# The first two weight chunks worked through together, piece by piece, and x loaded from a second queue

## The chip, the core and the metric

The kernel runs on one core of one Trainium2 chip. The metric is device time in microseconds (us) of one execution. The kernel before took 962.37 us (median of three runs, 961.73 to 966.79).

## What is computed

One layer of a streaming encoder on x, 512 tokens by 1024 channels, in float32. Cut to its shape:

```
proj = x @ w_in                       # 1024 columns in; queries, keys, values of four mixers, four gates out
o_a = top-k gathered softmax attention, chosen by an indexer (aiq, aik, aiw)
o_b = chunked attention with clipped relative bias
o_c = sliding window attention with sinks
o_d = stick-breaking attention
y   = sum over the four of sigmoid(gate_i) * (o_i @ w_branch_i)
x   = layer_norm(ALPHA * x + y @ w_out)
x   = layer_norm(ALPHA * x + (silu(hg) * hu) @ w_ffn_out)      # hg, hu = x @ w_ffn_in
```

## The kernel before

**Weights as a stream.** All weights come as 71 chunks of 1 MB, `stream[c]`, each 128 partitions by 2048 floats. A chunk of the input projection holds 256 output columns for all eight 128-row tiles of the contraction (`KT` = 8), 256 floats (`CW`) for each. Chunk 0 (`iq`) and chunk 1 (`ikck`) make indexer queries and keys, chunk 2 (`cvw`) values, chunk 3 `aq`, 4 `ak`, 5 `av`, 6 `dq`, and so on. Slot t is the work on chunk t.

**Three products for one.** For accuracy each float32 operand is split in two. ScalarE copies a chunk to `w_hi`, rounded (`high`, line 467); VectorE subtracts to get `w_lo` (`low`, line 701); TensorE multiplies hi by hi, hi by lo and lo by hi (`PARTS`). A chunk of the input projection is 48 matmuls: 2 output tiles, 8 contraction tiles, 3 parts. x itself is split once in the same way, into `x_hi` (line 597) and `x_lo` (line 856).

**Two buffers.** `raw`, `w_hi` and `w_lo` have two halves, chunk c in half c % 2. This makes a ring of waits:

- SyncE issues the load of chunk c into `raw` (line 353) once `low(c-2)` has read the half;
- ScalarE starts `high(c)` once the load has landed (`raw_loaded`) and once TensorE is done with chunk c-2 (`wait_used`, which waits for the last output tile of that chunk in `tile_done`);
- VectorE starts `low(c)` after `high(c)`, TensorE its slot c after `low(c)`.

On ScalarE each slot t does `high(t + 1)` ahead of emptying the output banks of chunk t (`empty_tile`, line 498 and others).

**The start.** Chunk 0 and x are cut in five `PIECES` along the contraction: tiles 0, 1, then 2-3, 4-5, 6-7. SyncE issues a piece of chunk 0 (line 342) and the same piece of x (line 343) in turn, ten DMAs, then chunk 1 whole (line 344). ScalarE and VectorE split piece by piece (lines 595, 597, 854, 856). TensorE first runs 11 matmuls on zeros (`WARM_UP`), and then chunk 0 tile by tile of the contraction (`first_chunk`, line 1051). Chunk 1 comes after it as an ordinary slot (`slot_half`, line 1027). The load of chunk 2 waits for the last `w_lo` piece of chunk 0, that of chunk 3 for `low(1)`.

**Beside it.** GpSimd computes small bias vectors and writes them to DRAM, every row repeated 128 times: `vec_t5` from 8 partitions (line 406, 2560 KB) and `vec_rel` from 4 partitions (line 407, 1280 KB). When both have landed it reads them back as bias tiles (line 411). These stores share the DMA engines with the weight stream.

The waits that order the loads in SyncE's loop:

```python
if j:
    sp.wait_ge(lo_ready, c - 1)
else:
    sp.wait_ge(first_lo_ready, len(PIECES))
    sp.wait_ge(lo_ready, c - 2)
```

The functions that the change touches:

Of the kernel before, what the change touches and what calls it, by code (L numbers as in the profile page):

```python
# [20 lines left out]
P = 128  # L21
# [14 lines left out]
KT = D_MODEL // P  # L36
TOK = SEQ // P
CHUNK_COLS = 2048
CW = CHUNK_COLS // KT
# [18 lines left out]
N_SLOTS = len(SLOTS)  # L58

PIECES = [(0, 1), (1, 2)] + [(k, k + 2) for k in range(2, KT, 2)]  # L60
OUT0 = N_SLOTS
FIN0 = OUT0 + 4
# [96 lines left out]
def layer_program(nc, stream, xT, x, t5T, relR, sinks, g1c, b1c, g1, b1, g2, b2, out):  # L159
# [96 lines left out]
    with ctx:  # L256
# [3 lines left out]
        def sem(name):  # L260
            return ctx.enter_context(nc.semaphore(name))

        raw_loaded = [sem("raw_loaded_even"), sem("raw_loaded_odd")]
        first_loaded = [sem(f"first_loaded{i}") for i in range(len(PIECES))]
        first_hi_ready, first_lo_ready = sem("first_hi_ready"), sem("first_lo_ready")
        x_loaded = [sem(f"x_loaded{i}") for i in range(len(PIECES))]
        sink_loaded, resid_loaded = sem("sink_loaded"), sem("resid_loaded")
        ln1_loaded, ln2_loaded, cols_loaded = sem("ln1_loaded"), sem("ln2_loaded"), sem("cols_loaded")
# [70 lines left out]
        @block.sync  # L339
        def _(sp):  # L340
            for i, (k, end) in enumerate(PIECES):
                sp.dma_start(raw[:, 0, CW * k:CW * end], stream[0, :, CW * k:CW * end]).then_inc(first_loaded[i], 16)
                sp.dma_start(xraw[:, k:end, :], xT[:, k:end, :]).then_inc(x_loaded[i], 16)
            sp.dma_start(raw[:, 1, :], stream[1]).then_inc(raw_loaded[1], 16)
            with sp.Fori(2, N_CHUNKS - 1, 2) as c:
                for j in range(2):

# [5 lines that stand above are left out]
                    sp.dma_start(raw[:, j, :], stream[bass.ds(c + j, 1)].rearrange("a p n -> p (a n)")).then_inc(raw_loaded[j], 16)  # L353
            for tok in range(TOK - 1):
                sp.wait_ge(out_ready, tok + 1)
                sp.dma_start(out[tok * P:(tok + 1) * P, :], result[:, tok, :]).then_inc(stored, 16)
            sp.wait_ge(out_ready, TOK)
            sp.dma_start(out[P * (TOK - 1):, 0:512], result[:, TOK - 1, 0:512]).then_inc(stored, 16)
            sp.wait_ge(stored, 16 * (TOK + 1))
# [90 lines left out]
        def _(act):  # L450
# [10 lines left out]
            def high(c):  # L461

                s = c % 2
                act.wait_ge(raw_loaded[s], 16 * ((c + 1) // 2))
                if c >= 2:
                    wait_used(act, c - 2)
                act.activation(w_hi[:, s, :], raw[:, s, :], ACT.Copy).then_inc(hi_ready, 1)  # L467
# [105 lines left out]
            def stack_high(n):  # L573
# [14 lines left out]
                act.activation(k_stack[rows, :], k[rows, :], ACT.Copy)  # L588
                act.activation(k_stack[others, :], k[rows, :], ACT.Copy).then_inc(stack_hi_ready, 1)

            act.preload_act_table_set("natural_log_exp_and_others")
            for i, (k, end) in enumerate(PIECES):
                s = slice(CW * k, CW * end)
                act.wait_ge(first_loaded[i], 16)
                act.activation(w_hi[:, 0, s], raw[:, 0, s], ACT.Copy).then_inc(first_hi_ready, 1)
                act.wait_ge(x_loaded[i], 16)
                act.activation(x_hi[:, k:end, :], xraw[:, k:end, :], ACT.Copy).then_inc(x_hi_ready, 1)
            for t in range(N_SLOTS):
                before, now = UNIT_AT.get(t - 1), UNIT_AT.get(t)
                if now is not None and UNITS[now][:2] == ("D", 0):  # L600
                    act.wait_ge(consts_ready, 1)
                    for rounded, mask in ((neg_tri_r, neg_tri), (neg_all_r, neg_all)):
                        act.activation(rounded[:], mask[:], ACT.Copy)
                if before is not None and UNITS[before][0] != "I":
                    unit_stage2(before)
                high(t + 1)
                if t == N_SLOTS - 1:
                    for k in range(EARLY):
                        y_high(k)
                stack_high(UNIT_AT.get(t + 1))  # L610
                if now is not None:
                    unit_stage1(now, before)
                else:
                    unit_out(before)
                if SLOTS[t][0] != "W":
                    empty_tile(t, 0)
                if SLOTS[t] == ("W", BRANCH_ORDER[-1]):
                    for j in range(EARLY, 8):
                        empty_tile(t, j)
                elif SLOTS[t][0] != "W" and t < N_SLOTS - 1:  # L620
                    empty_tile(t, 1)
# [33 lines left out]
            def high_of(c, s, loads, used, count):  # L655

                act.wait_ge(raw_loaded[s], loads * 16)
                act.wait_ge(used, count)
                act.activation(w_hi[:, s, :], raw[:, s, :], ACT.Copy).then_inc(hi_ready, 1)  # L659

            def ffn_pair(p, parity, first=False, early=False):
                if first:
                    high(FIN0 + 1)
                else:
                    high_of(FIN0 + 1 + 2 * p, (FIN0 + 1) % 2, p + (FIN0 + 2) // 2, up_done, 2 * p)
                for j in range(2):
                    act.wait_ge(gate_done, 2 * p + (j + 1))
                    if not first:
                        act.wait_ge(h_lo_ready, 2 * p + (j - 1))
                    act.activation(swi[:, j, :], banks[4 * parity + j][:], ACT.Tanh, scale=0.5).then_inc(tanh_ready, 1)  # L670
                high_of(FIN0 + 2 + 2 * p, FIN0 % 2, p + (FIN0 + 3) // 2, gate_done, 2 * p + 2)
                for j in range(2):
                    act.wait_ge(hidden_ready, 2 * p + (j + 1))
                    act.activation(h_hi[:, bass.ds(2 * p + j, 1), :], swi[:, j:j + 1, :], ACT.Copy).then_inc(h_hi_ready, 1)  # L674
# [11 lines left out]
        def _(dve):  # L686
# [164 lines left out]
            for i, (k, end) in enumerate(PIECES):  # L851
                s = slice(CW * k, CW * end)
                dve.wait_ge(first_hi_ready, i + 1)
                dve.tensor_tensor(w_lo[:, 0, s], raw[:, 0, s], w_hi[:, 0, s].bitcast(f32), ALU.subtract).then_inc(first_lo_ready, 1)
                dve.wait_ge(x_hi_ready, i + 1)
                dve.tensor_tensor(x_lo[:, k:end, :], xraw[:, k:end, :], x_hi[:, k:end, :].bitcast(f32),
                                  ALU.subtract).then_inc(x_lo_ready, 1)
            for t in range(N_SLOTS):
                before, now = UNIT_AT.get(t - 1), UNIT_AT.get(t)
                if now is not None and UNITS[now][0] == "A":  # L860
                    mask_unit(now)
                branch = BRANCH_ORDER.index(SLOTS[t][1]) if SLOTS[t][0] == "W" else None
                if branch is None:
                    low(t + 1)
                last_branch = branch == len(BRANCH_ORDER) - 1
                if branch is not None:
# [148 lines left out]
        def _(pe):  # L1015
# [23 lines left out]
                    e = EMPTIED_BY[g - 4]  # L1039
                    pe.wait_ge(act_emptied if e == "act" else dve_emptied, emptied_before(e, g - 4) + 1)  # L1040

            def first_chunk():

                for k in range(KT):
                    piece = next(i for i, (_, end) in enumerate(PIECES) if k < end)
                    pe.wait_ge(first_lo_ready, piece + 1)
                    pe.wait_ge(x_lo_ready, piece + 1)
                    for j in range(2):
                        w = columns(0, P * j, P, CW)
                        for n, (a, b) in enumerate(PARTS):  # L1050
                            ins = pe.matmul(prod[j][:], w[a](k), x_all[b](k), start=k == 0 and n == 0,  # L1051
                                            stop=k == KT - 1 and n == len(PARTS) - 1)
                        if k == KT - 1:
                            ins.then_inc(tile_done, 1)

            def slot_half(t, half, between=None):
                kind, what = SLOTS[t]
# [100 lines left out]
            pe.wait_ge(warm_ready, 1)  # L1158
            for _ in range(WARM_UP):
                pe.matmul(obank[:], warm[:, 0:P], warm[:], start=True, stop=True)  # L1160
            first_chunk()
            for t in range(1, N_SLOTS):
                before, now = UNIT_AT.get(t - 1), UNIT_AT.get(t)
                if before is not None and UNITS[before][0] != "I":
                    unit_stage2(before)
                pe.wait_ge(lo_ready, t)

                def units():
                    if now is not None:
                        unit_scores(now)  # L1170
                    if before is not None and UNITS[before][0] != "I":
                        unit_values(before)

                slot_half(t, 0, units)
                slot_half(t, 1)
# [146 lines left out]
```

## Time and profile before

| | |
|---|---|
| median of three runs | 962.37 us |
| span of the profiled execution, first to last instruction | 957.6 us |
| TensorE (PE) busy | 900.7 us, 94% |
| VectorE (DVE) busy | 466.3 us, 49% |
| ScalarE (ACT) busy | 339.7 us, 35% |
| GpSimd (POOL) busy | 56.0 us, 6% |
| mean granted TensorE clock | 0.967 |
| chain that ended last, by engine | PE 82%, DMA 9%, DVE 6%, ACT 1%, issue 1% |

The profiled execution is known by its span; 4.8 us lie between it and the median of the timed runs. In the rows below, times are us from the span's start, L is a line of the kernel, PEld is the weight load of TensorE, and SPq is SyncE's queue. "[2.50 <-DVE x_lo L856]" means that the engine stood idle for 2.50 us and that this instruction of DVE ended the wait. "DMA to landing" is the time from issue until the last byte has landed. q1 is the hardware queue that SyncE issues to, q0 the queue of GpSimd.

### The profile page before, as it was taken

What the parts mean: (1) busy time and instruction counts of PE and PEld (TensorE: products, weight loads), DVE (VectorE), ACT (ScalarE), POOL (GpSimd) and SP (SyncE); (2) the same over time, 40 slices, a digit from 0 to 9 for tenths busy, and PEclk for the clock granted to TensorE, in tenths of its full rate; (3) what the DMA queues carried; (4) which work ended last, traced back from release to release, by engine and by line L of the source; (5) the groups of instructions that cost most, each with busy time, mean ns of one, the idle gap of its engine ahead of it and who ended that gap; (6) DMA issues with size and microseconds to landing.
All of it is one profiled execution on the core that took longest, in us unless ns stands there. A gap on an engine that the chain in (4) does not pass through costs nothing.

```text
span 957.6 us, 10388 instructions
## 1 busy us (share of the span) xinstructions
PE 900.7 (94%) x4079; PEld 718.4 (75%) x4079; DVE 466.3 (49%) x742; ACT 339.7 (35%) x503; POOL 56.0 (6%) x92
## 2 busy tenths in 40 slices
PE   7949499999999999999999986999999999999996
PEld 5836478787777777777788864888888888888885
DVE  4204159878554753963628259334333444312217
ACT  4203236666453544453234152232222322212112
POOL 8000010000000000000000028000000000000001
PEclk9977799999999999999999997999999999999998
DMA  7876472112111311221222611322232222322212
GB/s 230 116 92 93 61 255 88 44 45 85 48 44 48 105 68 45 88 88 44 88 89 95 229 73 39 137 88 89 94 124 89 88 88 89 117 102 88 88 45 88
DMA packets 16168, 88.93 MB, mean 93 GB/s; under 512 B 2940, under 2 KB 3200, under 8 KB 7296
## 3 DMA queue, kind: packets, MB, share of 16 engines
q1 hardware_dynamic: 11952, 77.34, 22.5%
q0 software_dynamic: 4032, 10.78, 7.8%
q8 instruction: 28, 0.46, 0.2%
q10 hardware_dynamic: 144, 0.26, 0.1%
q14 instruction: 12, 0.10, 0.0%
HBM read 82.33 MB, written 6.03 MB: 92 GB/s over the span
## 4 chain that ended last, share of the span: by engine, by line
PE 82%; DMA 9%; DVE 6%; ACT 1%; issue 1%; POOL 0%; SPq 0%; DVEq 0%; POOLq 0%
PE bank L1027 54%; PE bank L1182 16%; DMA raw<-in_stream 9%; PE bank L1153 4%; PE bank L1111 2%; DVE x_lo L959 2%; PE bank L1110 2%; PE bank L1140 1%; DVE w_lo L701 1%; PE bank L1127 1%; PE bank L1051 1%; DMA xraw<-in_xT 1%; DVE x1t L955 1%; ACT w_hi L467 1%; PE bank L1099 1%; PE bank L1244 1%
## 5 line engine op out<-in xcount | busy, mean ns | idle before, releaser
L701 DVE TENSOR_TENSOR w_lo<-raw,w_hi 128x2048 fp32r<-128x2048 f32 x69 | 158.1, 2291 | 268.9 <-ACT w_hi L467 246.3
L1027 PE MATMUL bank<-x_hi,w_hi 128*128 128x512 f32 x720 | 188.2, 400 | 29.7 <-DVE w_lo L701 28.7
L1027 PEld LDWEIGHTS bank<-x_hi,w_hi 128*128 128x128 f32 x720 | 134.7, 191 | 60.2 <-DVE w_lo L701 29.3
L1027 PE MATMUL bank<-x_lo,w_hi 128*128 128x512 f32 x720 | 179.8, 392 | 0.0
L1027 PE MATMUL bank<-x_hi,w_lo 128*128 128x512 f32 x720 | 178.3, 390 | 0.0
L1027 PEld LDWEIGHTS bank<-x_lo,w_hi 128*128 128x128 f32 x720 | 136.3, 189 | 29.1
L1027 PEld LDWEIGHTS bank<-x_hi,w_lo 128*128 128x128 f32 x720 | 135.6, 188 | 28.3
L467 ACT ACTIVATE w_hi<-raw 128x2048 fp32r<-128x2048 f32 x48 | 92.0, 1917 | 181.5 <-PE bank L1182 94.9
L1182 PE MATMUL bank<-w_lo,h_hi 128*128 128x512 f32 x176 | 56.8, 389 | 0.0
L1182 PE MATMUL bank<-w_hi,h_lo 128*128 128x512 f32 x176 | 56.8, 389 | 0.0
L1182 PE MATMUL bank<-w_hi,h_hi 128*128 128x512 f32 x176 | 56.7, 389 | 0.0
L486 ACT ACTIVATE gates<-bank 128x512 f32<-128x512 f32 x30 | 17.9, 598 | 90.7 <-PE bank L1027 84.1
L674 ACT ACTIVATE h_hi<-swi 128x512 f32 (+1 forms) x22 | 13.9, 632 | 95.5 <-DVE swi L971 95.5
L670 ACT ACTIVATE swi<-bank 128x512 f32<-128x512 f32 x22 | 13.2, 599 | 89.4 <-PE bank L1027 70.5
L971 DVE SCALAR_TENSOR_TENSOR swi<-swi,bank 128x512 f32<-128x512 f32 x22 | 15.1, 687 | 60.6 <-PE bank L1027 60.6
L965 DVE SCALAR_TENSOR_TENSOR swi<-swi,bank 128x512 f32<-128x512 f32 x22 | 15.1, 687 | 54.8 <-ACT swi L670 54.8
L659 ACT ACTIVATE w_hi<-raw 128x2048 fp32r<-128x2048 f32 x21 | 40.0, 1905 | 0.0
L1182 PEld LDWEIGHTS bank<-w_hi,h_lo 128*128 128x128 f32 x176 | 33.0, 188 | 6.9
L1182 PEld LDWEIGHTS bank<-w_lo,h_hi 128*128 128x128 f32 x176 | 33.0, 188 | 6.8
L1182 PEld LDWEIGHTS bank<-w_hi,h_hi 128*128 128x128 f32 x176 | 33.0, 188 | 6.8
L706 DVE SCALAR_TENSOR_TENSOR gates<-gates,bank 128x512 f32<-128x512 f32 x22 | 14.6, 684 | 31.4 <-PE bank L1027 31.2
L543 ACT ACTIVATE probs<-probs,neg_max 128x256 f32<-128x256 f32 (+3 forms) x48 | 25.1, 525 | 10.5 <-DVE neg_max L814 10.2
(213 smaller groups left out, 1083.6 us busy)
## 6 DMA issues: line engine op xcount, KB each, us to landing
raw<-in_stream SPq DMA_DIRECT2D x69, 1024.0 KB, 4.8
bias_vectors<-vec_t POOLq DMA_DIRECT2D x1, 2560.0 KB, 55.1
resid<-in_x POOLq DMA_DIRECT2D x1, 2048.0 KB, 8.2
xraw<-in_xT SPq DMA_DIRECT2D x3, 512.0 KB, 7.6
out<-result SPq DMA_DIRECT2D x3, 512.0 KB, 3.1
bias_vectors<-vec_rel POOLq DMA_DIRECT2D x1, 1280.0 KB, 102.6
bias_b<-bias_vectors POOLq DMA_DIRECT2D x1, 1024.0 KB, 6.0
bias_a<-bias_vectors POOLq DMA_DIRECT2D x1, 1024.0 KB, 12.0
```

The source lines that it names most:

```text
L467: act.activation(w_hi[:, s, :], raw[:, s, :], ACT.Copy).then_inc(hi_ready, 1)
L486: ins = act.activation(gates[:, 2 * quarter + j, :], src[:], ACT.Tanh, scale=0.5)
L543: last = act.activation(probs[:, s], probs[:, s], ACT.Exp, bias=neg_max[:, r:r + 1], accum_out=row_sum[:, r:r + 1])
L659: act.activation(w_hi[:, s, :], raw[:, s, :], ACT.Copy).then_inc(hi_ready, 1)
L701: dve.tensor_tensor(w_lo[:, s, :], raw[:, s, :], w_hi[:, s, :].bitcast(f32), ALU.subtract).then_inc(lo_ready, 1)
L959: dve.tensor_tensor(x_lo[:, k, :], x1t[:, k, :], x_hi[:, k, :].bitcast(f32), ALU.subtract).then_inc(x1_lo_ready, 1)
L965: dve.scalar_tensor_tensor(swi[:, j, :], swi[:, j, :], 1.0, banks[4 * parity + j][:], ALU.add, ALU.mult).then_inc(gated, 1)
L1027: ins = pe.matmul(dst, lhs[a](k), rhs[b](k), start=n == 0, stop=n == n_all - 1)
L1110: pe.matmul(dst, q_stack[:, queries], k_stack[:, k0:k0 + width], start=True, stop=False)
L1111: ins = pe.matmul(dst, q_stack[rows, queries], k_low[rows, k0:k0 + width], start=False, stop=True)
L1153: ins = pe.matmul(obank[rows, q0:q0 + width], value_head(kind, h, kb), probsT[:, b * 512 + col:b * 512 + col + width], start=kb == 0, stop ...
L1182: return pe.matmul(banks[2 * tok + half][:], left[a][:, k, P * tok:P * (tok + 1)], (w_hi, w_lo)[b][:, (c0 + j) % 2, first:first + 512], st ...
```

## The change

Chunks 0 and 1 are both cut in `PIECES`. SyncE issues the ten pieces in turn, chunk 0 then chunk 1 of each; the five pieces of x are issued by ScalarE ahead of its table load. ScalarE and VectorE split, for each piece, chunk 0, x and chunk 1. TensorE goes along the contraction once and does both chunks at each tile of it. `high(1)`, `low(1)` and slot 1 fall away from the loops; the last piece of chunk 1 counts as `hi_ready` and `lo_ready` 1. Since chunk 1 no longer counts in `raw_loaded[1]`, the waits for odd chunks count one load less.

```diff
         @block.sync
             for i, (k, end) in enumerate(PIECES):
-                sp.dma_start(raw[:, 0, CW * k:CW * end], stream[0, :, CW * k:CW * end]).then_inc(first_loaded[i], 16)
-                sp.dma_start(xraw[:, k:end, :], xT[:, k:end, :]).then_inc(x_loaded[i], 16)
-            sp.dma_start(raw[:, 1, :], stream[1]).then_inc(raw_loaded[1], 16)
+                for c in range(2):
+                    sp.dma_start(raw[:, c, CW * k:CW * end], stream[c, :, CW * k:CW * end]).then_inc(first_loaded[c][i], 16)
...
         @block.scalar
+            for i, (k, end) in enumerate(PIECES):
+                act.dma_start(xraw[:, k:end, :], xT[:, k:end, :]).then_inc(x_loaded[i], 16)
             act.preload_act_table_set("natural_log_exp_and_others")
             for i, (k, end) in enumerate(PIECES):
                 s = slice(CW * k, CW * end)
-                act.wait_ge(first_loaded[i], 16)
+                act.wait_ge(first_loaded[0][i], 16)
                 act.activation(w_hi[:, 0, s], raw[:, 0, s], ACT.Copy).then_inc(first_hi_ready, 1)
                 act.wait_ge(x_loaded[i], 16)
                 act.activation(x_hi[:, k:end, :], xraw[:, k:end, :], ACT.Copy).then_inc(x_hi_ready, 1)
+                act.wait_ge(first_loaded[1][i], 16)
+                act.activation(w_hi[:, 1, s], raw[:, 1, s], ACT.Copy).then_inc(
+                    hi_ready if end == KT else second_hi_ready, 1)
...
-                high(t + 1)
+                if t:
+                    high(t + 1)
...
         @block.vector
                                   ALU.subtract).then_inc(x_lo_ready, 1)
+                if end == KT:
+                    dve.wait_ge(hi_ready, 1)
+                else:
+                    dve.wait_ge(second_hi_ready, i + 1)
+                dve.tensor_tensor(w_lo[:, 1, s], raw[:, 1, s], w_hi[:, 1, s].bitcast(f32), ALU.subtract).then_inc(
+                    lo_ready if end == KT else second_lo_ready, 1)
...
-                if branch is None:
+                if branch is None and t:
                     low(t + 1)
...
         @block.tensor
-            def first_chunk():
+            def first_chunks():
                 for k in range(KT):
                     piece = next(i for i, (_, end) in enumerate(PIECES) if k < end)
+                    for c in range(2):
+                        if c == 0:
+                            pe.wait_ge(first_lo_ready, piece + 1)
+                            pe.wait_ge(x_lo_ready, piece + 1)
+                        elif piece == len(PIECES) - 1:
+                            pe.wait_ge(lo_ready, 1)
+                        else:
+                            pe.wait_ge(second_lo_ready, piece + 1)
+                        for j in range(2):
+                            w = columns(c, P * j, P, CW)
+                            for n, (a, b) in enumerate(PARTS):
+                                ins = pe.matmul(prod[2 * c + j][:], w[a](k), x_all[b](k), start=k == 0 and n == 0,
+                                                stop=k == KT - 1 and n == len(PARTS) - 1)
+                            if k == KT - 1:
+                                ins.then_inc(tile_done, 1)
...
-            first_chunk()
-            for t in range(1, N_SLOTS):
+            first_chunks()
+            for t in range(2, N_SLOTS):
```

## Rows read from the trace of the kernel before

**Rows 1.** The page's busy times of the engines.
```profile
PE 900.7 (94%) x4079; PEld 718.4 (75%) x4079; DVE 466.3 (49%) x742; ACT 339.7 (35%) x503; POOL 56.0 (6%) x92
```

**Rows 2.** The page's chain that ended last, by line, and one of its DMA issues.
```profile
PE bank L1027 54%; PE bank L1182 16%; DMA raw<-in_stream 9%; PE bank L1153 4%; PE bank L1111 2%; DVE x_lo L959 2%; PE bank L1110 2%; PE bank L1140 1%; DVE w_lo L701 1%; PE bank L1127 1%; PE bank L1051 1%; DMA xraw<-in_xT 1%; DVE x1t L955 1%; ACT w_hi L467 1%; PE bank L1099 1%; PE bank L1244 1%
...
bias_vectors<-vec_rel POOLq DMA_DIRECT2D x1, 1280.0 KB, 102.6
```

**Rows 3.** That chain in order of time, 0 to 180: start, length, what.
```profile
23.74 1.92 ACT w_hi L467
25.68 2.30 DVE w_lo L701
...
28.14 41.44 DMA raw<-in_stream
...
74.01 40.68 DMA raw<-in_stream
```

**Rows 4.** Timeline, 36 to 160: TensorE's two restarts. Start, length, engine, line.
```profile
73.90 2.92 PE L1027 MATMUL bank<-x_hi,w_hi 128*128 128x512 f32 x6 [15.90 <-DVE w_lo L701]
...
119.00 2.93 PE L1027 MATMUL bank<-x_hi,w_hi 128*128 128x512 f32 x6 [12.81 <-DVE w_lo L701]
```

**Rows 5.** Instructions of the tile xraw (ns min/median/max, starts), then timeline, 0 to 60.
```profile
L343 SPq DMA_DIRECT2D xraw<-in_xT x5: 425/432/2365, 1.3 to 7.1; - x5
...
9.41 0.63 ACT L595 ACTIVATE w_hi<-raw 128x512 fp32r<-128x512 f32 x1 [1.22 <-DMA raw<-in_stream]
...
13.19 0.47 PE L1051 MATMUL bank<-x_hi,w_hi 128*128 128x512 f32 x1 [2.50 <-DVE x_lo L856]
...
14.73 1.06 ACT L597 ACTIVATE x_hi<-xraw 128x1024 fp32r<-128x1024 f32 x1 [0.44 <-DMA xraw<-in_xT]
...
17.24 1.92 ACT L467 ACTIVATE w_hi<-raw 128x2048 fp32r<-128x2048 f32 x1 [1.46 <-DMA raw<-in_stream]
...
22.82 0.39 PE L1051 MATMUL bank<-x_hi,w_lo 128*128 128x512 f32 x1
...
23.20 1.16 POOL L406 DMA_DIRECT2D bias_vectors<-vec_t  x1 [0.30 <-POOL vec_rel L402]
...
33.71 1.08 PEld L1027 LDWEIGHTS bank<-w_hi,x_hi 128*128 128x128 f32 x8
```

**Rows 6.** Groups by line and shape, 0 to 17: the splits of 512 and 1024 columns.
```profile
L856 DVE TENSOR_TENSOR x_lo<-xraw,x_hi 128x1024 fp32r<-128x1024 f32 x3 | 3.7, 1226 | 1.4 <-ACT x_hi L597 1.4
L597 ACT ACTIVATE x_hi<-xraw 128x1024 fp32r<-128x1024 f32 x3 | 3.2, 1058 | 1.5 <-DMA xraw<-in_xT 1.5
L854 DVE TENSOR_TENSOR w_lo<-raw,w_hi 128x512 fp32r<-128x512 f32 x3 | 2.1, 684 | 1.2 <-ACT w_hi L595 1.2
L595 ACT ACTIVATE w_hi<-raw 128x512 fp32r<-128x512 f32 x3 | 1.9, 619 | 1.2 <-DMA raw<-in_stream 1.2
```

**Rows 7.** Line 353 by stretches: the loads of chunk 3 and of chunk 5.
```profile
L353 SPq DMA_DIRECT2D raw<-in_stream x1: 342/342/342, 21.7 to 21.7; - x1
DMA to landing us min/median/max: 4.9/4.9/4.9
...
L353 SPq DMA_DIRECT2D raw<-in_stream x1: 332/332/332, 39.0 to 39.0; - x1
DMA to landing us min/median/max: 44.8/44.8/44.8
```

**Rows 8.** DMA queues: 34 to 40 (first), 60 to 66 (two), 84 to 88 (last).
```profile
q0 software_dynamic: 60, 0.31, 69.6%
...
q0 software_dynamic: 62, 0.32, 65.4%
q1 hardware_dynamic: 32, 0.26, 10.3%
...
q0 software_dynamic: 21, 0.11, 47.8%
```

**Rows 9.** Windows: busy time by engine, granted clock, DMA share, GB/s of one stretch.
```profile
13.80:17.20 3.40, 3.40 (x10) 2.62 (x9) 3.05 (x3) 1.54 (x2) 3.00 (x6) 0.50 0.69 216
```

More of the change, by code:

```diff
@@ L263, in layer_program @@
         raw_loaded = [sem("raw_loaded_even"), sem("raw_loaded_odd")]
-        first_loaded = [sem(f"first_loaded{i}") for i in range(len(PIECES))]
+        first_loaded = [[sem(f"first_loaded{c}_{i}") for i in range(len(PIECES))] for c in range(2)]
         first_hi_ready, first_lo_ready = sem("first_hi_ready"), sem("first_lo_ready")
+        second_hi_ready, second_lo_ready = sem("second_hi_ready"), sem("second_lo_ready")
         x_loaded = [sem(f"x_loaded{i}") for i in range(len(PIECES))]
@@ L463, in high @@
                 s = c % 2
-                act.wait_ge(raw_loaded[s], 16 * ((c + 1) // 2))
+                act.wait_ge(raw_loaded[s], 16 * (c // 2))
                 if c >= 2:
@@ L670, in ffn_pair @@
                     act.activation(swi[:, j, :], banks[4 * parity + j][:], ACT.Tanh, scale=0.5).then_inc(tanh_ready, 1)
-                high_of(FIN0 + 2 + 2 * p, FIN0 % 2, p + (FIN0 + 3) // 2, gate_done, 2 * p + 2)
+                high_of(FIN0 + 2 + 2 * p, FIN0 % 2, p + (FIN0 + 2) // 2, gate_done, 2 * p + 2)
                 for j in range(2):
@@ L1040, in bank_free @@
                     pe.wait_ge(act_emptied if e == "act" else dve_emptied, emptied_before(e, g - 4) + 1)
-            def first_chunk():
+            def first_chunks():
                 for k in range(KT):
                     piece = next(i for i, (_, end) in enumerate(PIECES) if k < end)
[L1046 to L1054, printed above, removed]
+                    for c in range(2):
[13 more added lines that the diff above has]
+                                ins.then_inc(tile_done, 1)
             def slot_half(t, half, between=None):
```

## The prediction

> **What bounds the kernel now.** I read the busy times first: TensorE is busy for 900.7 of 957.6 us [rows 1]. So a start that feeds it sooner ought to pay, if nothing between start and end can swallow what it gains. The chain of waits by line says that something can: 9% of the span hangs on weight loads [rows 2]. In order of time these are two loads only. Chunk 4 is issued at 28.14 and takes 41.44 us; chunk 6 is issued at 74.01 and takes 40.68 us [rows 3]. TensorE stands idle for 15.90 us before it restarts on chunk 4 at 73.90, and for 12.81 us before chunk 6 at 119.00 [rows 4]. After that no load stands in the chain, so whatever moves the restart at 119.00 moves the end by as much.
>
> Why do they take 41 us when chunk 3, issued at 21.7, took 4.9 [rows 7]? GpSimd issues its bias vector stores from 23.20 on [rows 5]. From 34 to 40, with chunk 4's load outstanding, q0 holds 70% of the DMA time and q1 moves nothing; from 60 to 66 q0 moves 62 packets and q1 32 [rows 8]. A load issued into these stores waits long and then gets its packets between theirs. So what matters is when chunk 4 is issued. That is the end of a ring: TensorE ends chunk 0 (its last matmul starts at 22.82 [rows 5]), `high(2)` may overwrite its half of `w_hi` from 23.74, `low(2)` runs from 25.68, and then SyncE may issue chunk 4 [rows 3].
>
> By the trace q0's share is 65 to 70% until 66 and 48% at 84 to 88 [rows 8], as if the store from 8 partitions and the one from 4 held engines of their own, 12 of 16 and later 8. The Trainium skill's "DMA: Bandwidth & Descriptors", "Why a DMA increments its semaphore by 16 and not by 1", states this: a DMA uses the largest number of engines up to 16 that divides its slowest dimension. The trace agrees. It enters no term below.
>
> **The change, part by part.**
>
> *Matmuls.* None is added. Chunks 0 and 1 are 96 matmuls in both orders. From 22.82 to 33.71 TensorE does one last matmul of chunk 0 and the 48 of chunk 1 [rows 5], less one step: 0.227 us each.
>
> *When the pieces are ready.* TensorE restarts at 13.19 on the third piece (tiles 2-3) [rows 5]. I take it that the third piece decides again: behind it lie six tiles, 72 matmuls, 16.3 us, and pieces four and five are ready in time (ScalarE needs 0.62 + 1.06 + 0.62 us for each and VectorE 0.68 + 1.23 + 0.68 [rows 6], 2.6 us against 5.4 us of matmuls). The third piece is ready when its chunk 0 part and its x have landed and been split: landing L plus 0.62 + 1.06 + 1.23 [rows 6], 2.95 us with the hops.
>
> *L.* The bytes are the same, 4 MB. By the rows 1024 KB had landed at 9.41 (third piece of chunk 0), 3072 KB at 14.73 (last of x), all 4096 KB at 17.24 [rows 5], so 385 KB per us between the first two. Ahead of the third piece now lie chunk 1's first two pieces, and x runs beside the weights on a second queue. If both queues move bytes alike, 768 KB of each: 1536 KB, L = 10.7. If they take turns packet by packet, x, whose rows are twice as long or more, gets ahead: all of x (2048 KB) and 768 KB of weights, 2816 KB, L = 14.1. While the bias stores run, q1 and q0 do seem to take turns by packet [rows 8], which speaks for the later end. Against it I set up to a microsecond for the 2.37 us that one of SyncE's ten issues took, where the others took 0.43 [rows 5]; with five of them on ScalarE's queue this should shorten. I take L = 13.0. ScalarE loses about 2.2 us for its own five issues (0.43 us each) before the table load; its first activation is late by 1 us or so, which the wait for the third piece hides.
>
> The Trainium skill, in the same page under "Queues, rings and completion order", says that an engine round-robins between the queues with work at packet granularity; by it alone L is 14.1 and the sum 1.1 us larger. Under "Issuing engines are not separate DMA queues" it says that issuing from two engines saves only issue time, no bandwidth; this speaks against the change.
>
> *TensorE through both chunks.* The third piece is ready at 13.0 + 2.95 = 15.95. Then 16.3 us of matmuls, and the clock: after its 2.50 us of idling TensorE ran from 13.80 to 17.20 at a granted clock of 0.50, 1.2 GHz [rows 9]; 36 matmuls took 9.86 us from 13.19, 1.7 more than 36 x 0.227. I charge the same 1.7 once. Bounds: nothing, if the doubled work on pieces one and two fills the gap, or twice that, as it now has a longer gap. Both chunks end at 15.95 + 16.3 + 1.7 = 34.0. Before, chunk 1 ended at 33.71 [rows 5]. The gain of interleaving (12 matmuls, 2.7 us, move into idle time ahead of the third piece) is spent on the later piece.
>
> *What is worse.* Chunk 0 is no longer done 48 matmuls before chunk 1, but 6. Its last matmul starts 7 steps before 34.0, at 32.4, not at 22.82. Everything on the ring goes with it by 9.6 us: `high(2)` at 33.3, `low(2)` from 35.3 to 37.6, chunk 4's load at 37.7. TensorE, done at 34.0, waits 3.6 us for `low(2)`, a wait that did not exist before. Behind `high(2)` on ScalarE are queued the emptying of chunk 1's banks and `high(3)`; slots 2 and 3 lasted from 33.71 to 58.0, where the idling before 73.90 began [rows 4, 5], and these 24.3 us hide both.
>
> *Chunks 2 and 3.* Chunk 2 is issued after chunk 0's last `w_lo` piece, chunk 3 after chunk 1's. The splits after L = 13.0 take 7 us on ScalarE plus VectorE's tail, so chunk 3 goes out at 21.5 to 23, as now at 21.7; it still lands ahead of the stores. Cost nothing; if it does not, see the third rival.
>
> *Chunk 4 to chunk 6.* The wait in the stores is what the rows price: 41.44 and 40.68 us, for issues at different phases, 28 and 74. So chunk 4 lands at 79.2, TensorE restarts at 83.5, and chunk 6 is issued at 83.6 and lands at 124.3. Chunk 5, issued after `low(3)` about 41, lands 14.2 us after chunk 4 as before (39.0 + 44.8 against 69.6 [rows 3, 7]) and is in time. TensorE restarts on chunk 6 at 128.6, not 119.0. GpSimd's bias tiles are not read before slot 10, so they give nothing back, and nothing after is late next: the rest is TensorE's.
>
> *Sum.* 957.6 + 9.6 = 967.2 us of span; with the 4.8 us that lie between span and median of the runs, 972.0.
>
> Bounds of the shift. Below: TensorE fed without a gap from about 6.5 us (my estimate, from ScalarE's later first activation) needs 96 x 0.227 = 21.8, an end at 28.3 and a shift of 4; with L = 10.7 and no clock loss it is 5.5. Above: L = 14.1, a second stretch at half clock (1.7), 0.5 for a late ScalarE: 12.9. The later store lands 102.6 us after its issue behind 23.20 [rows 2, 5], at 127, after which a load no longer waits, so it can hardly grow much beyond.
>
> **The rivals.**
>
> 1. *A load issued later waits less* (faster). Perhaps 41 us is the price of a load that meets the stores' beginning, and one issued at 37.7, in their steady state, gets its turn at once, like chunk 5, which needed 14.2 us behind chunk 4. Then chunk 4 lands at about 55, TensorE goes through slots 2 and 3 until 62 and on without waiting, 12 us earlier than 73.90; if chunk 6 still takes 40.7 us from its issue at 62, TensorE restarts at 107: 12 us faster, 950. It decides in this direction once chunk 4 waits under 32 us. Against it: chunk 6, issued in the steady state, took 40.68.
> 2. *The landing is fixed by the stores, not by the issue* (no change). Chunk 4 then lands near 69.6 wherever it is issued before 45, and TensorE restarts at 73.90 and 119.00: 962. For it: no packet of q1 from 34 to 40. Against: the two waits are alike to 0.8 us though their ends lie 45 us apart.
> 3. *Chunk 3 meets the stores.* Issued after 24 it would land at 65; slot 3 ends at 83, chunk 6 is issued about 84 and lands at 125: 10 to 13 us slower, 974.
> 4. *Even pieces* (L near 10.7, clock kept): the mechanism of the forecast with a shift of 4 to 6, 967.
> 5. *The change does not do what it says*: the fine interleaving is in the program order of TensorE, so only the early landing can fail; that is inside the bounds of L.
>
> **How the numbers follow.** Forecast 0.58 (shift 6 to 13), rival 4 0.16, rival 3 0.06, rival 2 0.10, rival 1 0.07, others 0.03. Half a per cent, 4.8 us, is about what a measurement can tell from no change. Faster by more than that: rival 1, 0.08. Within it: rival 2 and the lowest tenth of rival 4 with others, 0.14. Slower: 0.78. The range reaches from just above rival 2, 963, to 977, the upper bound 975.3 with the spread of the runs; outside are rival 1, most of rival 2 and a few per cent above.
>
> **What would show it.** In the changed profile: TensorE's last matmul of the first two chunks near 34 and chunk 0's `tile_done` just before; an idle time of 3 to 4 us of TensorE ahead of slot 2; chunk 4 issued near 37.7 with 41 us to landing; restarts near 83.5 and 128.6; the rest of the trace equal to before but shifted. A landing of chunk 4 in under 32 us, or near 69.6, would make the prediction wrong at the fourth step; an end of the first chunks before 30 would make its size wrong.

## The result

The changed kernel takes 970.0 us (median of 20 runs, 966.66 to 978.33), the kernel before 964.61 us (median of 20, 958.68 to 970.85). The ratio is 1.0068, with a 95% interval from 1.0044 to 1.0091: slower by 0.7%, some 6.6 us. The three runs shown ahead of the prediction had a median of 962.37. (One correction to what stands above: the stream has 70 chunks, not 71.)

In the profiled execution the span is 970.1 us, against 957.6. The page of the changed kernel:

```profile
span 970.1 us, 10396 instructions
PE 909.9 (94%) x4079; PEld 727.7 (75%) x4079; DVE 466.8 (48%) x746; ACT 339.7 (35%) x507; POOL 55.9 (6%) x92
...
PE 81%; DMA 10%; DVE 6%; ACT 1%; issue 0%; POOL 0%; SPq 0%; DVEq 0%; POOLq 0%
```

TensorE has the same number of instructions as in [rows 1] but is busy for 9 us more: the same matmuls, slower. The share of loads in the chain rises from 9 to 10%. The chain that ended last, 0 to 200, in order of time (start, length, what), has the pieces of [rows 3] again:

```profile
2.68 10.79 DMA raw<-in_stream
13.50 0.63 ACT w_hi L597
14.13 0.96 ACT x_hi L599
15.11 1.24 DVE x_lo L862
16.48 15.26 PE bank L1069 x66
31.79 0.47 issue
32.27 1.91 ACT w_hi L467
34.20 2.30 DVE w_lo L707
36.66 42.53 DMA raw<-in_stream
79.22 1.92 ACT w_hi L467
81.16 2.30 DVE w_lo L707
83.62 41.04 DMA raw<-in_stream
```

The third piece's weights land at 13.5, its products start at 16.48. 66 matmuls later chunk 0 is complete; ScalarE empties its two banks and then starts `high(2)`. Chunk 4 is issued at 36.66, where [rows 3] has 28.14, and waits 42.53 us. The timeline of TensorE shows three waits for `w_lo`, where [rows 4] has two:

```profile
36.55 1.97 PE L1039 MATMUL bank<-w_hi,x_hi 128*128 128x132 f32 x8 [3.46 <-DVE w_lo L707]
...
128.97 2.93 PE L1039 MATMUL bank<-x_hi,w_hi 128*128 128x512 f32 x6 [14.30 <-DVE w_lo L707]
```

The first is new, ahead of slot 2. The second restart comes 10.0 us later than the 119.00 of [rows 4]. After it something more is lost. The windows (span, busy time by engine with the number of instructions, granted clock, DMA share, GB/s) of the changed kernel after that restart, and below them those of the kernel before:

```profile
129.00:141.30 12.30, 12.07 (x25) 7.82 (x26) 7.34 (x12) 4.88 (x8) 1.54 (x3) 0.51 0.94 352
```

```profile
119.00:123.00 4.00, 3.78 (x8) 2.23 (x8) 3.05 (x5) 1.51 (x4) 0.00 (x0) 0.50 0.85 183
123.00:134.40 11.40, 11.40 (x48) 8.87 (x49) 4.14 (x7) 3.65 (x5) 2.31 (x3) 1.00 0.66 232
```

TensorE had idled in both, and in both it restarted at a granted clock of 0.50, 1.2 GHz. But the kernel before got 2.4 GHz back after 4.0 us, the changed kernel after 12.3. Slot 7 starts at 147.91 instead of 134.36: 13.55 us late, 9.97 of it at the restart and 3.58 at the lower clock. About 1 us comes back by the end. The two spans differ by 12.5 us, the medians of 20 runs by 5.4: part of what this pair of profiles shows belongs to the two executions, and the experiments have to say which part.

### The profile page after: what moved, and what is told of

Same layout as the page of the kernel before. It is cut to its first block, busy times and chain, and to the rows that moved or that the text cites. A ratio compares the mean times of both kernels' runs of the same rounds, so it can differ in the third digit from the quotient of the medians.

```text
span 970.1 us, 10396 instructions
## 1 busy us (share of the span) xinstructions
PE 909.9 (94%) x4079; PEld 727.7 (75%) x4079; DVE 466.8 (48%) x746; ACT 339.7 (35%) x507; POOL 55.9 (6%) x92
## 4 chain that ended last, share of the span: by engine, by line
PE 81%; DMA 10%; DVE 6%; ACT 1%; issue 0%; POOL 0%; SPq 0%; DVEq 0%; POOLq 0%
PE bank L1039 54%; PE bank L1200 15%; DMA raw<-in_stream 10%; PE bank L1171 4%; PE bank L1129 2%; DVE x_lo L971 2%; PE bank L1128 2%; PE bank L1069 2%; PE bank L1158 1%; DVE w_lo L707 1%; PE bank L1145 1%; DVE x1t L967 1%; ACT w_hi L467 1%; PE bank L1117 1%; DVE resid L932 1%; PE bank L1262 0%
## 5 line engine op out<-in xcount | busy, mean ns | idle before, releaser
L707 DVE TENSOR_TENSOR w_lo<-raw,w_hi 128x2048 fp32r<-128x2048 f32 x68 | 155.8, 2292 | 279.7 <-ACT w_hi L467 257.0
L1039 PE MATMUL bank<-x_hi,w_hi 128*128 128x512 f32 x704 | 184.6, 401 | 27.4 <-DVE w_lo L707 26.4
L1039 PE MATMUL bank<-x_lo,w_hi 128*128 128x512 f32 x704 | 175.9, 392 | 0.0
L1039 PEld LDWEIGHTS bank<-x_hi,w_hi 128*128 128x128 f32 x704 | 131.9, 192 | 57.2 <-DVE w_lo L707 27.0
L1039 PE MATMUL bank<-x_hi,w_lo 128*128 128x512 f32 x704 | 174.3, 390 | 0.0
L1039 PEld LDWEIGHTS bank<-x_lo,w_hi 128*128 128x128 f32 x704 | 133.3, 189 | 28.4
L1039 PEld LDWEIGHTS bank<-x_hi,w_lo 128*128 128x128 f32 x704 | 132.6, 188 | 27.7
```

The source lines that it names most:

```text
L707: dve.tensor_tensor(w_lo[:, s, :], raw[:, s, :], w_hi[:, s, :].bitcast(f32), ALU.subtract).then_inc(lo_ready, 1)
L1039: ins = pe.matmul(dst, lhs[a](k), rhs[b](k), start=n == 0, stop=n == n_all - 1)
```

## The experiments

Each kernel is compared with runs of the kernel before on the same chip; ratios are to the kernel before. Where two kernels of different experiments are set side by side below, the kernel before took 964.94, 964.37 and 964.88 us on the three chips used.

**Both kernels once more.** One profile each had been read; how far does a second one differ?

> The kernel before, unchanged, for a second profile of it. Theory A (chunk 4 is issued at a time that the ring of buffers sets, and each load then waits some 41 us in the bias stores): chunk 4 is issued near 28.1, lands after 40 to 43 us, TensorE restarts near 74 and near 119 to 121; the ratio to itself is 1.000. Theory B (what differs from run to run is the clock after the restarts, not the loads): the stretches at a granted clock of 0.5 begin and end at other places than in the first profile, and the span differs from 957.6 by several us though the restarts stand within 2 us of the first profile's.

Measured: 961.84 us against 964.94 of the kernel before, ratio 0.9988 (0.9955 to 1.0021). Its chain, 0 to 180, then TensorE's second restart in the timeline and the window behind it:

```profile
14.83 10.03 PE bank L1051 x36
...
29.79 40.92 DMA raw<-in_stream
...
75.13 40.15 DMA raw<-in_stream
```

```profile
119.59 1.65 PE L1027 MATMUL bank<-x_hi,w_hi 128*128 128x512 f32 x3 [12.28 <-DVE w_lo L701]
```

```profile
119.60:131.00 11.40, 11.17 (x23) 7.12 (x24) 6.35 (x8) 4.56 (x8) 2.32 (x3) 0.50 0.71 200
```

The third piece starts at 14.83, where [rows 5] has 13.19, and chunk 4 goes out at 29.79, not 28.14. The waits of 41 us are the same. The clock stayed at 1.2 GHz for 11.4 us behind the restart, where the first profile had 4.0.

> The changed kernel, unchanged, for a second profile of it. Theory A: chunk 4 is issued at 36 to 38, the restarts come at 83 to 84 and 128 to 130, about 10 us behind the kernel before. If the end moves by much less than 10 us in the timed runs (ratio 1.004 to 1.009), the difference lies after the second restart (clock) or in chunk 6, whose landing the end of the stores near 125 cuts short when the kernel before lands it late. Theory B: the second restart is 10 us late in this profile too and the clock stretches differ from the first profile's by up to 4 us of matmul time.

Measured: 971.35 us, ratio 1.0078 (1.0049 to 1.0107). Its chain:

```profile
36.12 44.85 DMA raw<-in_stream
...
85.39 43.83 DMA raw<-in_stream
```

The issue falls into the expected 36 to 38; the waits are 2 to 3 us longer here and put the second restart at 133.54, later than the expected 128 to 130. It also shows that the end of the stores cuts nothing short. Over two profiles each, chunk 4 is issued at 28.14 and 29.79 before, at 36.66 and 36.12 after: 7.4 us later on the mean, 8.5 in the first pair. As to the clock, three of the four profiles agree and the first one of the kernel before is the exception with its 4.0 us. In after_again the window behind the second restart reads:

```profile
133.50:144.70 11.20, 10.94 (x22) 6.98 (x23) 7.27 (x12) 4.94 (x8) 2.32 (x3) 0.50 0.91 320
```

So the 3.6 us after the restart belong to an execution, not to the kernel. In before_again, though, the restarts do stand within 2 us of the first profile's, as theory B said.

**Without the bias stores.** If the stores are the amplifier, taking them away should leave little of the loss.

```diff
-            pool.dma_start(vec_dram[0:2 * HEADS], vec_t5[:]...).then_inc(vec_stored, 16)
-            pool.dma_start(vec_dram[2 * HEADS:], vec_rel[:]...).then_inc(vec_stored, 16)
-            pool.wait_ge(vec_stored, 32)
...
-                pool.dma_start(tile[:], ...).then_inc(bias_loaded, 16)
-            pool.wait_ge(bias_loaded, 16 * 3)
+            for t in ("B", "C"):
+                pool.memset(bias[t][:], 0.0)
+            step(pool.memset(bias["A"][:], 0.0))
+            step_wait()
```

> The kernel before without the stores of the bias vectors and without reading them back; the bias tiles are filled with zeros, so the outputs are not the reference's. Theory A: no load takes more than 6 us, TensorE does not idle before slots 4 and 6, and 28.7 us of idling and some 10 us at half clock go: 925 to 935 us. Rival (the loads are slow for another reason): under 5 us faster.

Measured: 924.31 us, ratio 0.9588 (0.9555 to 0.9622), just below the expected range. TensorE waits for no `w_lo` of a whole chunk any more, and chunk 4 lands 4.8 us after its issue.

> The same with the changed kernel (no bias stores, zeros in the bias tiles, outputs not the reference's). Theory A: what the change costs without the stores is only the later start of slot 2, near 36 instead of 33.7, since TensorE waits for low(2) for 3.6 us after the first chunks: 1.5 to 3 us slower than the kernel before without stores. Rival (the delay of the ring costs 10 us by itself, stores or not): 8 to 10 us slower than it. Rival that the change was meant for (interleaving gains when loads are fast): 0 to 3 us faster than it.

Measured: 936.51 us. That is 12.2 us slower than before_nostore, and my expectation of 1.5 to 3 was wrong by a factor of four or more. The rival of 8 to 10 us from the ring does not fit either: slot 2 starts at 38.37, 2.5 us behind the 35.88 of before_nostore. The window from there on, in after_nostore, shows the rest:

```profile
38.30:62.10 23.80, 23.73 (x103) 22.63 (x103) 4.40 (x5) 5.44 (x9) 0.00 (x0) 0.50 0.24 89
```

After 3.5 us of waiting TensorE ran at 1.2 GHz for 23.8 us. This I call theory C: the short wait ahead of slot 2 costs more by the clock behind it than by itself. In the changed kernel the same stretch is there; I took it to be hidden, because slots 2 and 3 end before chunk 4 lands in any case (after_fill, below, tests this). The changed kernel's window:

```profile
35.50:59.40 23.90, 22.85 (x102) 22.43 (x103) 4.65 (x4) 3.88 (x6) 0.00 (x0) 0.51 0.81 86
```

**Only the later issue of chunk 4.** The step on which the prediction rests, done alone in the kernel before.

```diff
-            with sp.Fori(2, N_CHUNKS - 1, 2) as c:
+            ...                                    # chunks 2 and 3 as before, written out
+            sp.wait_ge(tile_done, 4)
+            with sp.Fori(4, N_CHUNKS - 1, 2) as c:
```

> The kernel before, with one wait added: SyncE issues chunk 4 only when TensorE has ended chunk 1 (tile_done 4). Nothing else moves. Theory A (the time of chunk 4's issue sets the restarts): chunk 4 is issued at 34 to 36 instead of 28 to 30, lands 41 to 44 us later, both restarts and the end come 5 to 6 us later: ratio 1.005 to 1.006. Rival (landing is fixed by the stores): chunk 4 lands near 70 all the same, ratio 1.000.

Measured: 972.67 us, ratio 1.0071 (1.0035 to 1.0106). Its chain and its second restart:

```profile
35.82 43.20 DMA raw<-in_stream
...
83.45 42.09 DMA raw<-in_stream
```

```profile
129.86 2.93 PE L1032 MATMUL bank<-x_hi,w_hi 128*128 128x512 f32 x6 [14.80 <-DVE w_lo L706]
```

One wait on SyncE, with nothing else changed, costs as much as the whole change: 6.8 us, with an interval from 3.4 to 10.2. The landing moved with the issue, so it is not fixed by the stores. In this profile the second restart is 10 us late and not 5 to 6, because both loads also waited longer, 43.20 and 42.09 us.

**Only TensorE's order undone.**

```diff
-                for k in range(KT):
-                    for c in range(2):
+                for c in range(2):
+                    for k in range(KT):
```

> The changed kernel with one part undone: TensorE does all of chunk 0 and then all of chunk 1; loads, queues and splits stay interleaved. Theory A (the loss comes from chunk 0 ending only 6 matmuls before chunk 1): chunk 0's last matmul starts near 24.5 to 25, high(2) near 25.5, chunk 4 is issued near 30, TensorE does not wait ahead of slot 2, restarts near 76 and 121, time within 2 us of the kernel before: ratio 0.999 to 1.003. Rival (the loads in smaller pieces and the busier ScalarE are what costs): ratio stays at 1.006 or more.

Measured: 965.69 us, ratio 1.0022 (0.9992 to 1.0052), no longer told from the kernel before. Its chain:

```profile
16.59 11.12 PE bank L1069 x36
27.75 0.47 issue
28.22 1.92 ACT w_hi L467
...
32.63 41.18 DMA raw<-in_stream
```

Chunk 4 goes out at 32.63, 2.6 us later than expected: the third piece is ready at 16.59, and its 36 matmuls took 11.12 us instead of 10.0, at half clock for part of it. By the medians the order of the matmuls is the larger part of the loss and the interleaved loads, which make the third piece late, a smaller one; the interval here and that of the change (1.0044 to 1.0091) overlap a little.

Put together, the runs give a series of chunk 4's issue against the ratio:

| kernel | chunk 4 issued | ratio |
|---|---|---|
| before, two profiles | 28.14, 29.79 | 1 (0.9988) |
| after_chunk0_first | 32.63 | 1.0022 |
| before_hold4 | 35.82 | 1.0071 |
| changed, two profiles | 36.66, 36.12 | 1.0068, 1.0078 |
| after_fill (below) | 37.70 | 1.0075 |

From 29 to 36.4 that is 7.4 us of issue for 6.6 to 7.5 us of time. The series is good to some 3 us at each point, not better: every ratio has an interval of about 0.3% to either side, and in the profiles the waits of chunks 4 and 6 in the stores varied between 40.1 and 44.9 us. The longer waits do not go with the later issue: after_fill, with the latest issue of all, has 41.57 and 40.1.

**The stores done otherwise.** If 41 us of waiting come from the way in which the stores go out, in rows of 2.5 KB from 8 and 4 partitions, one wide transfer of the same copies should take it away, with the right outputs.

```diff
-            pool.dma_start(vec_dram[0:2 * HEADS], vec_t5[:].unsqueeze(1).to_broadcast([2 * HEADS, P, VL])).then_inc(vec_stored, 16)
-            pool.dma_start(vec_dram[2 * HEADS:], vec_rel[:].unsqueeze(1).to_broadcast([HEADS, P, VL])).then_inc(vec_stored, 16)
-            pool.wait_ge(vec_stored, 32)
+            pool.dma_start(vec_small[0:2 * HEADS], vec_t5[:]).then_inc(small_stored, 16)
+            pool.dma_start(vec_small[2 * HEADS:], vec_rel[:]).then_inc(small_stored, 16)
+            pool.wait_ge(small_stored, 32)
+            pool.dma_start(vec_dram[:], bass.AP(vec_small.tensor, vec_small.offset, [[0, P], [1, 3 * HEADS * VL]])).then_inc(vec_stored, 16)
+            pool.wait_ge(vec_stored, 16)
```

`vec_dram` is now 128 rows of 12 x 640 floats, and the readback steps by 12 x 640 - 1.

> The kernel before with the bias stores done otherwise: the 12 vectors are stored once (30 KB), and one transfer from DRAM to DRAM, 128 rows of 30 KB, makes the 128 copies, so that no store goes out from 8 or 4 partitions. Same outputs. Theory A: chunk 4 lands in under 20 us, TensorE's idling before slots 4 and 6 goes wholly or nearly, 925 to 940 us. Rival (it is the bytes of the stores, not their few source partitions): the loads stay slow, over 950 us.

Measured: 923.62 us (921.74 to 925.13), ratio 0.9561 (0.9532 to 0.9590). It beats both kernels by over 40 us and is as fast as with no stores at all. Among its DMA issues (what, engine, count, KB, us to landing) is the one that makes the copies:

```profile
bias_vectors<-bias_small POOLq DMA_DIRECT2D x1, 3840.0 KB, 16.3
```

The two stores before needed 102.6 us for the same 3840 KB. [rows 2] puts that time against the 1280 KB alone, but both stores count on one semaphore, so it tells only when the later of them had landed. Chunk 4's load, issued at 29.2 beside the wide transfer, still took 17.0 us instead of 4.8. That costs nothing, because TensorE has slots 2 and 3 to work on meanwhile and the transfer is over soon.

What about the stores was slow? The edit changes three things at once: the engines that the copies are spread over, the bytes in one packet, and the memory that they are read from (DRAM and not SBUF). The queue view separates the first. This is GpSimd's queue from 30 to 36 in before_spread (packets, MB, share of the 16 engines' time):

```profile
q0 software_dynamic: 54, 1.66, 78.3%
```

[rows 8] has 60 packets, 0.31 MB and 69.6% for six microseconds of the old stores. So the queue holds hardly more of the engines' time than before, and its packets take about as long, 1.4 us against 1.1 (share times 16 engines times 6 us, over the packets). But each carries 31 KB and not 5. Even after one of the old stores had landed, when the queue was down to 47.8% [rows 8], the share is a factor of 1.6; the bytes in a packet are a factor of six. The few partitions, and the few engines that go with them, are therefore the smaller part of the slowness. Whether a packet of 5 KB needs 1.1 us for its short rows or for being read from SBUF was not tested.

> The changed kernel with the same other stores. After the runs without stores I expect the changed kernel to be 10 to 13 us slower than before_spread: 2 us of later start of slot 2 and some 10 us of half clock after its 3.5 us wait ahead of slot 2. If the clock stays up, 2 to 3 us slower.

Measured: 938.40 us (935.29 to 939.00), 14.8 us above before_spread, a little more than expected. These two kernels scatter by 4 us, not 12, so the parts can be read. TensorE's timeline at slot 2, first before_spread, then after_spread:

```profile
35.02 1.01 PE L1030 MATMUL bank<-w_hi,x_hi 128*128 128x132 f32 x8
35.86 1.06 PE L1030 MATMUL bank<-w_lo,x_hi 128*128 128x132 f32 x8
```

```profile
39.61 1.83 PE L1042 MATMUL bank<-w_hi,x_hi 128*128 128x132 f32 x8 [3.46 <-DVE w_lo L710]
41.24 1.91 PE L1042 MATMUL bank<-w_lo,x_hi 128*128 128x132 f32 x8
```

Slot 2 starts 4.6 us later, after a wait of 3.46 us, and then eight products take 1.91 us instead of 1.06. The rest, about 10 us, is the stretch that begins there. The window of after_spread:

```profile
39.60:63.50 23.90, 23.89 (x104) 22.75 (x104) 4.69 (x4) 5.66 (x9) 3.90 (x8) 0.50 0.60 222
```

TensorE is busy all the time and has 1.2 GHz.

**The wait filled.** Theory C, tested: TensorE is kept at work through the wait.

```diff
             first_chunks()
+            for _ in range(14):
+                pe.matmul(obank[:], x_hi[:, 0, 0:P], x_hi[:, 0, :], start=True, stop=True)
```

> after_spread with 14 matmuls more, whose result nobody reads, in TensorE's 3.5 us wait ahead of slot 2. They take 14 x 0.227 = 3.2 us, so slot 2 starts as before near 39.6. Theory C (the wait costs 3.5 us itself and 10 to 12 us by the half clock that follows it): the stretch at 0.5 from 39.9 goes, slot 2 takes 10.9 us instead of 20.4, 938.4 falls to 926 to 929 us. Rival (the clock falls for another reason, as slot 2's short matmuls): no change, 938.

Measured: 927.05 us, 11.4 us less than after_spread, by doing more. Its timeline, and the window from 34 on:

```profile
34.64 3.33 PE L1184 MATMUL bank<-x_hi 128*128 128x512 f32 x14
38.26 1.11 PE L1042 MATMUL bank<-w_hi,x_hi 128*128 128x132 f32 x8 [0.29 <-DVE w_lo L710]
39.21 1.06 PE L1042 MATMUL bank<-w_lo,x_hi 128*128 128x132 f32 x8
```

```profile
34.00:60.00 26.00, 25.71 (x159) 21.97 (x158) 10.70 (x10) 12.40 (x18) 3.91 (x8) 1.00 0.92 317
```

The half clock is gone, with the same short matmuls in slot 2, so these did not bring it about. What is left of the change is 3.4 us, and slot 2 starts 3.2 us later than in before_spread.

> The changed kernel, with its bias stores as they are, and the same 14 matmuls more ahead of slot 2. Theory C with theory A: the half clock in slots 2 and 3 goes, but these slots end before chunk 4 lands anyway, so the restarts and the time stay: ratio to the kernel before 1.004 to 1.010. Rival (the half clock is part of the loss that was timed): ratio near 1.000.

Measured: 971.39 us, ratio 1.0075 (1.0047 to 1.0103). Slots 2 and 3 run at full clock (the window), chunk 4 waits 41.57 us as ever (the chain), and TensorE idles for longer instead, 21.84 us ahead of the first restart where the changed kernel has 12.10:

```profile
36.00:60.50 24.50, 24.21 (x152) 20.73 (x151) 5.20 (x4) 4.42 (x7) 0.00 (x0) 1.00 0.80 86
```

```profile
37.70 41.57 DMA raw<-in_stream
```

So in the changed kernel as it stands the half clock at slot 2 costs nothing, and the ring's delay behind the stores is the loss.

**The parts of the change with the wide transfer.**

> after_chunk0_first (loads and splits interleaved, TensorE does chunk 0 first) with the single wide bias transfer. No wait ahead of slot 2, so no half clock after it. Theory C: within 3 us of before_spread's 923.6, on the slow side since the third piece is ready 1 to 2 us later (16.6 against 14.3): 924 to 927. If the interleaved loads themselves cost more, 930 or above.

Measured: 926.07 us (924.99 to 927.54), 2.4 us above before_spread: what the interleaved loads cost when TensorE takes chunk 0 first.

> before_spread with one part of the change alone: x is issued from ScalarE's queue, chunk 1 whole as before. If the queues take turns packet by packet, x gets ahead of chunk 0's pieces, and the third piece (x lands last now, at about 11.9) is ready 1 us earlier to 1 us later: 922.5 to 925. If the second queue brings bandwidth, 921 or below.

Measured: 922.89 us (921.94 to 923.90), 0.7 us below before_spread, within the scatter of both. Its chain has the third piece at work at 12.82, where before_spread has 14.32:

```profile
9.84 0.63 ACT w_hi L599
10.47 0.96 ACT x_hi L601
11.45 1.24 DVE x_lo L860
12.82 10.03 PE bank L1055 x36
```

The second queue for x is thus no part of the loss. That it makes the start earlier is not shown: 1.5 us in one profile, where five profiles with the opening of the kernel before (13.19, 14.83, 14.50, 14.57 and 14.32) differ by 1.6, and 0.7 us in the timed runs.

## Why the prediction was right, point by point

The sign, the mechanism and the range were right. The size was not as right as it looks. The sum was forecast as 972.0 and measured as 970.0, but from another baseline: I forecast a shift of 9.6 us, and the timed runs show 5.4 between the medians and 6.6 by the ratio. The shift was thus 3 to 4 us too large, and the baseline of three runs, 962.37, was 2.2 us below the 964.61 of twenty. That the second error covered half of the first was luck.

- *The ring.* Right. before_hold4 makes a loss of the same size by one wait, and after_chunk0_first undoes most of it by the order of the matmuls alone. Forecast for chunk 4's issue 37.7, measured 36.66 and 36.12.
- *L, and the third piece.* L was taken as 13.0 between 10.7 and 14.1; it was 13.5, and 12.98 in the second profile. By the rule of the Trainium skill's "DMA: Bandwidth & Descriptors", "Queues, rings and completion order" (an engine goes round-robin between its queues, packet by packet) it would have been 14.1; the traces came 0.6 and 1.1 us before that, nearer to it than to 10.7. They also show x ahead, as that end supposes: in the changed kernel ScalarE waits for pieces of the weights only, never for x. My support for it from [rows 8] was misread: 62 packets against 32, and 60 against none, are no turns one for one. The products started at 16.48, not 15.95.
- *The shift of the ring.* This is the term that was mis-sized: 9.6 us forecast, 7.4 measured over two profiles each. At the late end chunk 4's issue came 1.3 us before the 37.7, mostly since the clock's 1.7 us (next point) did not fall due. At the early end I took the third piece's start before as 13.19, from the one profile there was. It is 14.83 in before_again, 14.50 in before_hold4 and 14.32 in before_spread; that first profile caught x early.
- *The clock's 1.7 us.* Charged to the stretch behind the third piece; it did not fall there. The window 11.60 to 15.00 of the changed kernel has a granted clock of 0.54, but that is during the second piece, and TensorE still had to wait 0.37 us for the third, so it cost nothing. The 66 matmuls from 16.48 took 15.26 us, at full clock. In after_spread, with the same opening, it did fall behind the third piece: there the 66 took 18.00 us.
- *The wait ahead of slot 2.* Forecast 3.6 us, measured 3.46. That it is followed by 23.9 us at half clock I did not see. Chunk 4's load hid it here; without the stores it is the dearest part of the change.
- *41 us of waiting.* 42.53 and 41.04 in the profile, 44.85 and 43.83 in the second: right to 4 us.
- *The rest shifted.* Wrong by 3.6 us in the profiled execution, from the clock after the second restart. The span came out as 970.1, not 967.2. In before_again there is such a long stretch as well (11.4 us), so I do not count it as a difference of the kernels.
- *Chunk 3* landed 7.0 us after its issue at 21.8, before the stores took hold: rival 3 did not come. Rival 1 falls with the waits of 41 us and more, rival 2 with before_hold4, rival 4 with L at 13.0 to 13.5.

What stays open is why a load needs 41 us there and not 15. That it hangs on how these stores are done is shown (before_spread), and that their few engines are not the main reason is read from the packets; which property of them it is, and how an engine divides its time between the two queues, no run here separated. The gain that the change was meant to bring, an earlier start, came in no run: with the stores done otherwise and the wait filled it still costs 3.4 us.

## What to carry to other kernels

Two buffers worked through in step are freed in step. Before two generations of a double buffer are merged to fill a gap at the start, look for who waits for the first one to come free, and what that load will meet when it goes out 7 us later. And where a load takes eight times its usual time, mend that first: it was worth 41 us here, while the new start as a whole gained nothing in any run. After any new wait of a few microseconds on TensorE, look at the granted clock behind it before you price it.

## What the runs showed of the hardware

- A wait of 3.5 us on TensorE cost about 10 us more through the granted clock: 0.50 for 23.8 us after it, with TensorE busy all the time. In the first profile of the kernel before, after 12.8 us of idling, 4.0 us at half clock were all; in the second it was 11.4, in the changed kernel 12.3 and 11.2. What sets the length was not separated. Fourteen matmuls that compute nothing of use in the gap won 11.4 us.
- 3840 KB of copies took over 100 us as two stores from 8 and 4 partitions of SBUF, and 16.3 us as one transfer from DRAM to DRAM with 128 rows of 30 KB. A packet took 1.1 us with 5 KB in the first case and 1.4 us with 31 KB in the second. Beside the two stores a weight load took 30 to 58 us instead of 4.8 (all kernels that have them; 8.7 for one issued at 119.1, as they ended); beside the one transfer it took 17.0.
- With the wide transfer the timed runs lay within 3.4 us (6 runs) instead of 12.2 (20 runs of the kernel before).
